# A two-block forward pass: four plain feature tiles ahead of the second feed-forward's seven-product stage, and three low halves of its activation sums made by GpSimd

## The chip, the core and the metric

The kernel runs on one core of a Trainium2 chip. The metric is the time of the device in microseconds (us), from the first to the last instruction of the program with the little that lies around it; lower is better. The engines of the core are named as in the profile: PE is the matrix engine (TensorE), PEld its weight loads, DVE is VectorE, ACT is ScalarE, POOL is GpSimd, SP (SyncE) issues most of the transfers.

## What is computed

The program is a forward pass of two blocks over 512 tokens of width 1024, all in float32. The first block has a modulated RMS norm, a convolution branch, a chunked mLSTM and a feed-forward. The second block has retention and latent attention, a feed-forward and a gated embedding. The change touches the feed-forward of the second block alone:

```
hn = rmsnorm(h, pre_ffn_norm[i])
ff = (jax.nn.silu(hn @ w_gate[i]) * (hn @ w_up[i])) @ w_down[i]
h = h + rmsnorm(ff, post_ffn_norm[i])
```

`hn` is 512 x 1024, `w_gate` and `w_up` are 1024 x 2816, so 22 feature tiles of 128 columns each.

## The kernel before

**Precision.** A float32 product is made of three passes. Each operand is split into a high half (`sph` for weights, `HH` for activations) and a low half, which is what is left of it (`spl`, `HL`), and PE adds high x high, low x high and high x low. ACT makes the high half of a weight tile by a copy, DVE the low half by a subtraction. A tile's row may hold several buffers of the same name (`raw`, `sph`, `spl`, `sums`): weights land in four `raw` buffers, their halves go into three `sph` and `spl` buffers.

**Plain feature tiles.** For feature tile f a unit of `w_gate` and a unit of `w_up` (128 x 1024 each) are multiplied with all 512 tokens: 24 matmuls of 512 columns for each, `hl` at lines 1884 and 1885 and `lo` at line 1892. DVE takes the gate out of its bank (`up_gate`, L2817), ACT applies silu and later rounds the product to `midh` (L2342), DVE multiplies (`up_`, L2828), and POOL makes the low half `midl` (L3169).

**Seven-product feature tiles.** For the other features, gate and up weights are seen as a 2 x 2 block (gate or up, first or second half of the 1024 inputs) and the activations as a 2 x 2 block (half of the inputs, half of the tokens). Their product is made of seven block products in place of eight, each of 12 matmuls of 256 columns (`seven`, L1922, L1924 and L1932), which is 84 matmuls for a feature. `SEVEN[2] = (5, 22)` says that features 5 to 21 of the second block go this way and 0 to 4 the plain way. `SEVEN_STEP` is the order in which the seven products of a feature are made. Each product needs

- its weight operand: the bare halves of a `raw` buffer or sums of them. A feature takes one accumulating transfer on POOL's queue (`seven_third`, L3130) and three sums on DVE (`seven_sum`, L2772, L2775, L2778), then a high half on ACT (`seven_high`, L2284) and a low half on DVE (`seven_low`, L2788) for each of the seven;
- its activation operand: bare quarters of `HH` and `HL`, or one of four sums of quarters. These four are made once for the stage: the sum `ts` on DVE (`seven_t_sum`, L2751 to L2759), its high half `th` on ACT (`seven_t_high`, L2272), its low half `tl` on DVE (`seven_t_low`, L2764), each 128 x 1024. `tl` lies where its `ts` lay, for number 0 to 2. `ts` 1 is worked out from `ts` 0, and `ts` 3 from `ts` 1. Products 1, 2, 4 and 6 of a feature (counted from 0 in the order made) use activation sums 0, 1, 2 and 3.

**What sets the order.** `plan()` writes one list of steps, and each engine runs its own steps of that list in this order; semaphores do the rest. `halves_2(n)` is called after plain tile n (even: gate, odd: up) has been taken out of its bank, and puts the steps for the activation sums between the plain tiles. The first five plain tiles (three gates and two ups) are multiplied before any is taken out, the normalising row of all tokens being late; the others follow one by one. A weight unit's `raw` buffer is loaded again once both halves of what was in it are made.

The plain tiles of this stage are multiplied from about 1140 us on, the seven-product features from 1191.15 us to 1362.68 us, and then `w_down` follows.

Of the kernel before, what the change touches and what calls it, by code (L numbers as in the profile page):

```python
# [7 lines left out]
ALU = mybir.AluOpType  # L8
ACT = mybir.ActivationFunctionType
AX = mybir.AxisListType  # L10
F32 = mybir.dt.float32
# [51 lines left out]

MIX_WORK = (2, 3)

SEVEN = {1: (3, 22), 2: (5, 22)}
SEVEN_STEP = (0, 3, 2, 4, 5, 1, 6)
SEVEN_SUMS = (2, 3, 4)

# [19 lines left out]
class Signals:  # L89
# [11 lines left out]
    def up(self, name, *labels, by=1):  # L101
        self.count[name] = self.count.get(name, 0) + by
        for label in labels:
            assert label not in self.now, label
            self.now[label] = (name, self.count[name])
        return self.sem(name), by

    def at(self, *label):
        if not self.known:
            return None  # L110
        name, value = self.known[label]
        return self.sem(name), value
# [18 lines left out]
def plan():  # L131
# [750 lines left out]
    def begin_seven(which):  # L882
        f0, f1 = SEVEN[which]
        st = {"which": which, "first": W["used"] + 2 * f0 + sum(st["slots"] - st["units"] for st in stages), "units": 2 * (f1 - f0),
# [77 lines left out]
    def ffn_up(which, acts, names, hook=None):  # L962
# [18 lines left out]
        for i in range(NFT):  # L981
            jobs += part(i)
        f0, f1 = SEVEN[which]

        def halves_2(n):
            if n in (2 * f0 - 4, 2 * f0 - 2):
                add("seven_third", which, (n - 2 * f0 + 4) // 2)
            if n == 0:
                add("seven_t_sum", which, 0)
                add("seven_t_high", which, 0)  # L990
            elif n == 2:
                ready()
                add("seven_t_sum", which, 1)
                add("seven_t_low", which, 0)
                add("seven_t_high", which, 1)
            elif n == 3:
                add("seven_t_sum", which, 3)
            elif n == 4:
                ready(more=1)
                add("seven_t_low", which, 1)  # L1000
            elif n == 5:
                add("seven_t_sum", which, 2)
                add("seven_t_high", which, 2)
            elif n == 6:
                add("seven_t_low", which, 2)

        def halves(n):
# [494 lines left out]
def program(nc, A, out, known):  # L1502
    steps, units = plan()
    ctx = ExitStack()
    with ctx:
        G = Signals(lambda name: ctx.enter_context(nc.semaphore(name)), known)
        up, at = G.up, G.at
# [44 lines left out]
        TH, TL, TS = [], [], []  # L1552
# [907 lines left out]
        def _(e):  # L2460
            w = Waited(e, G)
            up, fence = follow("DVE")
# [297 lines left out]
                ins.then_inc(*up("s_cut", ("seven_t_sum", which, t)))  # L2760

            def seven_t_low(which, t):
                w.wait_ge(at("seven_t_high", which, t))
                e.tensor_tensor(TL[t], TS[t][:], TH[t].bitcast(F32),  # L2764
                                ALU.subtract).then_inc(*up("s_cut", ("seven_t_low", which, t)))
# [329 lines left out]
        def _(e):  # L3095
            w = Waited(e, G)
            up, fence = follow("POOL")
# [23 lines left out]
            def x_reload(which, half):  # L3121
# [2 lines left out]
                e.dma_start(XT[:, 4 * half:4 * half + 4, :], A["x_scratch"][:, 4 * half:4 * half + 4, :]).then_inc(  # L3124
                    *G.up(f"d_xb{half}", ("x_back", which, half), by=16))

            def seven_third(which, i):
                n = seven_at[which][0] + 2 * i
                w.wait_ge(at("raw", n), at("raw", n + 1))
                e.dma_start(raw_half(n + 1, 0), raw_half(n, 0), accum_op=ALU.add).then_inc(  # L3130
                    *G.up(f"d_third{i % 2}", ("seven_third", which, i), by=16))
# [47 lines left out]
            def mix_ret():  # L3179
                for h in (1, 3):  # L3180
# [2 lines left out]
                        *up("s_cut_p", ("lo", "mix", h)))  # L3183

            run({"begin": begin, "zero_pads": zero_pads, "split": split, "sum": total, "v_begin": v_begin, "decay_begin": decay_begin, "m_out": m_out, "m_rows": m_rows,
                 "x_reload": x_reload, "seven_third": seven_third, "seven_mid_low": seven_mid_low,
                 "normlo": normlo, "up": up_, "rope_full": rope_full, "mix_ret": mix_ret,
                 "fence": fence})

# [129 lines left out]
```

## Time and profile before

| | us |
|---|---|
| median of three runs | 1541.39 |
| the three runs | 1541.39, 1543.04, 1539.12 |
| the profiled execution | 1539.65 |
| its span, first to last instruction | 1537.5 |
| PE busy | 1516.3 (99%) |
| DVE busy | 1136.2 (74%) |
| ACT busy | 799.4 (52%) |
| POOL busy | 150.3 (10%) |

The span is what the trace covers; the execution's own time has 2.15 us more. The shares are averages over a program of many stages, so that a stage is read from its own rows. A matmul's row has a length that reaches beyond the start of the next one, since matmuls are pipelined: what a matmul costs is read from the starts of two rows.

### The profile page before, as it was taken

What the parts mean: (1) busy time and instruction counts of PE and PEld (TensorE: products, weight loads), DVE (VectorE), ACT (ScalarE), POOL (GpSimd) and SP (SyncE); (2) the same over time, 40 slices, a digit from 0 to 9 for tenths busy, and PEclk for the clock granted to TensorE, in tenths of its full rate; (3) what the DMA queues carried; (4) which work ended last, traced back from release to release, by engine and by line L of the source; (5) the groups of instructions that cost most, each with busy time, mean ns of one, the idle gap of its engine ahead of it and who ended that gap; (6) DMA issues with size and microseconds to landing.
All of it is one profiled execution on the core that took longest, in us unless ns stands there. A gap on an engine that the chain in (4) does not pass through costs nothing.

```text
span 1537.5 us, 21554 instructions
## 1 busy us (share of the span) xinstructions
PE 1516.3 (99%) x8220; PEld 1290.2 (84%) x8220; DVE 1136.2 (74%) x1842; ACT 799.4 (52%) x1281; POOL 150.3 (10%) x158
## 2 busy tenths in 40 slices
PE   8999999999999999999999999999999999999998
PEld 3788777777788899999888887778888999998877
DVE  8999988898887789977673546766577888854356
ACT  5545477764553656666433335446455666643223
POOL 0111000000000101111021011010202111100100
PEclk9999999999999999999999999999999999999999
DMA  9788221223566546666623323111325565573331
GB/s 370 183 189 208 75 85 63 88 83 101 201 237 212 167 116 189 197 159 165 187 95 103 110 85 110 62 49 36 108 84 190 145 163 144 158 247 103 100 137 69
DMA packets 66344, 214.10 MB, mean 139 GB/s; under 512 B 7741, under 2 KB 10045, under 8 KB 65218
## 3 DMA queue, kind: packets, MB, share of 16 engines
q1 hardware_dynamic: 52496, 179.68, 34.2%
q0 software_dynamic: 13744, 33.04, 11.3%
q8 instruction: 65, 1.06, 0.3%
q14 instruction: 37, 0.30, 0.1%
q10 hardware_dynamic: 2, 0.00, 0.0%
HBM read 175.99 MB, written 8.40 MB: 120 GB/s over the span
## 4 chain that ended last, share of the span: by engine, by line
PE 84%; DVE 9%; ACT 4%; issue 2%; DMA 1%; ACTq 0%; DVEq 0%; SPq 0%
PE bank L1884 16%; PE bank L1892 16%; PE bank L1885 16%; PE bank L1922 8%; PE bank L1932 8%; PE bank L1924 8%; PE bank L1950 2%; DVE convout L2538 2%; PE bank L1962 1%; PE bank L1964 1%; PE bank L1963 1%; DVE spl L2476 1%; PE bank L2054 1%; PE bank L2067 1%; PE bank L2037 1%
## 5 line engine op out<-in xcount | busy, mean ns | idle before, releaser
L1884 PE MATMUL bank<-HH,sph 128*128 128x512 f32 x856 | 343.7, 402 | 5.6 <-DVE spl L2476 1.7
L1885 PE MATMUL bank<-HH,spl 128*128 128x512 f32 x856 | 333.9, 390 | 0.0
L2476 DVE TENSOR_TENSOR spl<-raw,sph 128x1024 fp32r<-128x1024 f32 (+1 forms) x165 | 205.1, 1245 | 165.5 <-ACT sph L2112 165.2
L2112 ACT ACTIVATE sph<-raw 128x1024 fp32r<-128x1024 f32 (+1 forms) x185 | 189.0, 1025 | 150.8 <-PE bank L1892 117.5
L1892 PE MATMUL bank<-HL,sph 128*128 128x512 f32 x856 | 226.1, 396 | 0.0
L1884 PEld LDWEIGHTS bank<-HH,sph 128*128 128x128 f32 x856 | 160.8, 188 | 45.9 <-issue 7.8
L1885 PEld LDWEIGHTS bank<-HH,spl 128*128 128x128 f32 x856 | 160.8, 188 | 34.7 <-issue 1.7
L1892 PEld LDWEIGHTS bank<-HL,sph 128*128 128x128 f32 x856 | 159.6, 188 | 34.6 <-issue 1.4
L2538 DVE SCALAR_TENSOR_TENSOR convout<-convin,vecs,convout 128x512 f32<-128x512 f32 x240 | 166.0, 742 | 0.0
L1922 PE MATMUL bank<-HH,sph 128*128 128x256 f32 x576 | 144.7, 283 | 0.1
L1924 PE MATMUL bank<-HH,spl 128*128 128x256 f32 x576 | 144.4, 283 | 0.0
L1884 PE MATMUL bank<-midh,sph 128*128 128x512 f32 x352 | 137.1, 389 | 0.0
L1885 PE MATMUL bank<-midh,spl 128*128 128x512 f32 x352 | 137.0, 389 | 0.0
L1922 PEld LDWEIGHTS bank<-HH,sph 128*128 128x128 f32 x576 | 110.5, 192 | 0.6 <-ACT tmp L2294 0.3
L1924 PEld LDWEIGHTS bank<-HH,spl 128*128 128x128 f32 x576 | 110.5, 192 | 0.1
L1922 PE MATMUL bank<-th,sph 128*128 128x256 f32 x432 | 108.4, 283 | 0.2 <-ACT tmp L2289 0.2
L1924 PE MATMUL bank<-th,spl 128*128 128x256 f32 x432 | 108.3, 283 | 0.0
L2788 DVE TENSOR_TENSOR spl<-raw,sph 128x512 fp32r<-128x512 f32 x144 | 97.1, 694 | 11.8 <-ACT sph L2284 11.7
L2284 ACT ACTIVATE sph<-sums 128x512 fp32r<-128x512 f32 x108 | 63.4, 622 | 69.7 <-DVE sums L2775 69.7
L1932 PE MATMUL bank<-HL,sph 128*128 128x256 f32 x576 | 92.6, 283 | 0.0
L2284 ACT ACTIVATE sph<-raw 128x512 fp32r<-128x512 f32 x144 | 89.7, 624 | 4.6 <-PE bank L1932 1.2
L1892 PE MATMUL bank<-midl,sph 128*128 128x512 f32 x352 | 87.6, 389 | 0.0
(365 smaller groups left out, 2688.3 us busy)
## 6 DMA issues: line engine op xcount, KB each, us to landing
raw<-in_w_in SPq DMA_DIRECT2D x69, 512.0 KB, 3.2
raw<-in_w_up SPq DMA_DIRECT2D x66, 512.0 KB, 4.4
more<-in_w_ada SPq DMA_DIRECT2D x32, 512.0 KB, 5.7
raw<-in_w_down SPq DMA_DIRECT2D x32, 512.0 KB, 3.7
raw<-in_w_gate SPq DMA_DIRECT2D x22, 512.0 KB, 3.5
raw<-raw POOLq DMA_DIRECT2D x36, 256.0 KB, 4.4
midl<-tmp POOLq DMA_DIRECT2D x36, 256.0 KB, 3.3
spl<-raw POOLq DMA_DIRECT2D x17, 512.0 KB, 5.5
```

Of the source, the lines that this page charges most:

```text
L1884: e.matmul(P_[b][:], sph(n)[:, q], hi[:, k, :], start=k == 0, stop=False)
L1885: e.matmul(P_[b][:], spl(n)[:, q], hi[:, k, :], start=False, stop=False)
L1892: m = e.matmul(P_[b][:], sph(n)[:, q], low[:, k, :], start=False, stop=last and k == kb - 1)
L1922: e.matmul(to, high_of(which, s)[:, q], x, start=begins and k == 0, stop=False, skip_group_check=not begins)
L1924: e.matmul(to, low_of(which, s)[:, q], x, start=False, stop=False, skip_group_check=not begins)
L1932: m = e.matmul(to, high_of(which, s)[:, q], x, start=False, stop=k == 3, skip_group_check=not begins)
L1950: m = e.matmul(P_[b][:], raw(n)[:, token(k)], FULL[acts][:, k, :], start=k == 0, stop=k == 7)
L2112: e.activation(sph(n), raw(n), ACT.Copy).then_inc(*up("s_w_high", ("wh", n)))
L2284: e.activation(high_of(which, s), given, ACT.Copy).then_inc(*up("s_w_high", ("seven_high", which, s), *labels))
L2476: e.tensor_tensor(spl(n), raw(n), sph(n).bitcast(F32), ALU.subtract).then_inc(*up("s_w_low", ("wl", n)))
L2538: ins = e.scalar_tensor_tensor(CO[:, i, :], src, wt, CO[:, i, :], ALU.mult, ALU.add)
L2788: e.tensor_tensor(low_of(which, s), given, high_of(which, s).bitcast(F32), ALU.subtract).then_inc(*up("s_w_low", ("seven_low", which, s), ...
```

## The change

`SEVEN[2]` becomes `(4, 22)`: feature 4 is made by seven products and no longer by two plain tiles, so the stage has four plain features and eighteen of the other kind. `halves_2` puts the low half of activation sum 2 with its sum and high half, at n = 5, where it stood at n = 6. The low halves of activation sums 0, 1 and 2 move from DVE to POOL, with waits on the sums that read the same memory before it is overwritten. In the first feed-forward nothing changes.

```diff
-SEVEN = {1: (3, 22), 2: (5, 22)}
+SEVEN = {1: (3, 22), 2: (4, 22)}
+POOL_LOWS = (0, 1, 2)
...
             elif n == 5:
                 add("seven_t_sum", which, 2)
                 add("seven_t_high", which, 2)
-            elif n == 6:
                 add("seven_t_low", which, 2)
...
             def seven_t_low(which, t):
+                if which == 2 and t in POOL_LOWS:
+                    return
                 w.wait_ge(at("seven_t_high", which, t))
...
+            def seven_t_low(which, t):
+                if which == 2 and t in POOL_LOWS:
+                    w.wait_ge(at("seven_t_high", which, t))
+                    if t < 2:
+                        w.wait_ge(at("seven_t_sum", which, (1, 3)[t]))
+                    e.tensor_tensor(TL[t], TS[t][:], TH[t].bitcast(F32),
+                                    ALU.subtract).then_inc(*up("s_cut_p", ("seven_t_low", which, t)))
```

The last function stands among POOL's steps.

On DVE, from activation sum 1 (`ts_101`) on, before; `tmp` rows take plain tiles out of their banks, `spl` rows of 128x1024 belong to plain units:

```order
L2754 SCALAR_TENSOR_TENSOR ts_101<-pf,ts_98 128x1024
L2764 TENSOR_TENSOR tl_97<-ts_98,th_96 128x1024
L2828 TENSOR_TENSOR tmp_91<-tmp_91,bank 128x512
L2759 SCALAR_TENSOR_TENSOR ts_105<-pf,ts_101 128x1024
L2817 TENSOR_TENSOR tmp_90<-bank,rrow 128x512
L2476 TENSOR_TENSOR spl_63<-raw_56,sph_60 128x1024
L2764 TENSOR_TENSOR tl_100<-ts_101,th_99 128x1024
L2828 TENSOR_TENSOR tmp_90<-tmp_90,bank 128x512
L2756 TENSOR_TENSOR ts_104<-pf 128x1024
L2476 TENSOR_TENSOR spl_61<-raw_57,sph_58 128x1024
L2817 TENSOR_TENSOR tmp_87<-bank,rrow 128x512
L2764 TENSOR_TENSOR tl_103<-ts_104,th_102 128x1024
```

and after:

```order
L2754 SCALAR_TENSOR_TENSOR ts_101<-pf,ts_98 128x1024
L2830 TENSOR_TENSOR tmp_91<-tmp_91,bank 128x512
L2759 SCALAR_TENSOR_TENSOR ts_105<-pf,ts_101 128x1024
L2819 TENSOR_TENSOR tmp_90<-bank,rrow 128x512
L2476 TENSOR_TENSOR spl_63<-raw_56,sph_60 128x1024
L2830 TENSOR_TENSOR tmp_90<-tmp_90,bank 128x512
L2756 TENSOR_TENSOR ts_104<-pf 128x1024
L2790 TENSOR_TENSOR spl_61<-raw_57,sph_58 128x512
L2819 TENSOR_TENSOR tmp_87<-bank,rrow 128x512
L2774 TENSOR_TENSOR sums_65<-raw_54 128x512
L2777 TENSOR_TENSOR sums_64<-sums_65,raw_57 128x512
L2780 TENSOR_TENSOR sums_65<-raw_57,sums_65 128x512
```

The three `tl` rows are gone, and behind activation sum 2 (`ts_104`) the operands of the first seven-product feature follow at once.

On POOL, from the low half of plain feature 0 (`midl<-tmp_89`) on, before; the DMA rows are the accumulating transfers of `seven_third`:

```order
L3169 TENSOR_TENSOR midl<-tmp_89,midh 128x512
L3169 TENSOR_TENSOR midl<-tmp_91,midh 128x512
L3169 TENSOR_TENSOR midl<-tmp_90,midh 128x512
L3130 DMA raw_56<-raw_55 128x512
L3169 TENSOR_TENSOR midl<-tmp_87,midh 128x512
L3130 DMA raw_54<-raw_57 128x512
L3169 TENSOR_TENSOR midl<-tmp_86,midh 128x512
```

and after:

```order
L3179 TENSOR_TENSOR midl<-tmp_89,midh 128x512
L3134 TENSOR_TENSOR tl_97<-ts_98,th_96 128x1024
L3179 TENSOR_TENSOR midl<-tmp_91,midh 128x512
L3140 DMA raw_54<-raw_57 128x512
L3134 TENSOR_TENSOR tl_100<-ts_101,th_99 128x1024
L3179 TENSOR_TENSOR midl<-tmp_90,midh 128x512
L3134 TENSOR_TENSOR tl_103<-ts_104,th_102 128x1024
L3140 DMA raw_56<-raw_55 128x512
L3179 TENSOR_TENSOR midl<-tmp_87,midh 128x512
```

The low halves of the activation sums now stand between those of the plain features, and the first accumulating transfer stands two places earlier.

On ACT, from the high half of activation sum 2 (`th_102`) on, before:

```order
L2272 ACTIVATE th_102<-ts_104 128x1024
L2112 ACTIVATE sph_58<-raw_57 128x1024
L2335 ACTIVATE tmp_87<-tmp_87 128x512
L2112 ACTIVATE sph_59<-raw_54 128x1024
L2342 ACTIVATE midh<-tmp_87 128x512
L2284 ACTIVATE sph_60<-raw_55 128x512
L2335 ACTIVATE tmp_86<-tmp_86 128x512
```

and after:

```order
L2272 ACTIVATE th_102<-ts_104 128x1024
L2284 ACTIVATE sph_58<-raw_57 128x512
L2335 ACTIVATE tmp_87<-tmp_87 128x512
L2284 ACTIVATE sph_58<-sums_64 128x512
L2284 ACTIVATE sph_59<-sums_65 128x512 x2
L2284 ACTIVATE sph_60<-raw_54 128x512
L2342 ACTIVATE midh<-tmp_87 128x512
```

The high half of the first seven-product operand (`sph_58<-raw_57`, 128x512) is now the next instruction behind `th_102`.

## Rows read from the trace of the kernel before

**Rows 1.** The page: the span, and the granted PE clock in 40 slices

```profile
span 1537.5 us, 21554 instructions
...
PEclk9999999999999999999999999999999999999999
```

**Rows 2.** Timeline of PE: start us, length us, line, operation, count, [idle before <-releaser]

```profile
1174.01 0.47 PE L1884 MATMUL bank<-HH,sph 128*128 128x512 f32 x1
...
1177.73 1.98 PE L1892 MATMUL bank<-HL,sph 128*128 128x512 f32 x8
1180.18 0.47 PE L1884 MATMUL bank<-HH,sph 128*128 128x512 f32 x1 [0.47 <-DVE spl L2476]
...
1183.89 1.98 PE L1892 MATMUL bank<-HL,sph 128*128 128x512 f32 x8
1185.71 0.39 PE L1884 MATMUL bank<-HH,sph 128*128 128x512 f32 x1
...
1191.15 0.28 PE L1922 MATMUL bank<-HH,sph 128*128 128x256 f32 x1
...
1192.58 0.28 PE L1922 MATMUL bank<-th,sph 128*128 128x256 f32 x1
...
1362.68 0.40 PE L1884 MATMUL bank<-midh,sph 128*128 128x512 f32 x1
```

**Rows 3.** Timeline of DVE in the plain tiles and the first seven-product operands

```profile
1165.21 1.21 DVE L2754 SCALAR_TENSOR_TENSOR ts<-pf,ts 128x1024 f32<-128x1024 f32 x1
1166.34 2.32 DVE L2764 TENSOR_TENSOR tl<-ts,th 128x1024 fp32r<-128x1024 f32 x1
1168.58 0.67 DVE L2828 TENSOR_TENSOR tmp<-tmp,bank 128x512 f32<-128x512 f32 x1
...
1172.64 1.23 DVE L2476 TENSOR_TENSOR spl<-raw,sph 128x1024 fp32r<-128x1024 f32 x1 [1.65 <-ACT sph L2112]
1173.78 1.22 DVE L2764 TENSOR_TENSOR tl<-ts,th 128x1024 fp32r<-128x1024 f32 x1
...
1185.32 1.38 DVE L2788 TENSOR_TENSOR spl<-raw,sph 128x512 fp32r<-128x512 f32 x1 [1.22 <-ACT sph L2284]
...
1187.22 0.68 DVE L2772 TENSOR_TENSOR sums<-raw 128x512 f32<-128x512 f32 x1
...
1189.39 1.89 DVE L2788 TENSOR_TENSOR spl<-sums,sph 128x512 fp32r<-128x512 f32 x3
...
1197.10 0.69 DVE L2772 TENSOR_TENSOR sums<-raw 128x512 f32<-128x512 f32 x1
```

**Rows 4.** Timeline of POOL in the same stretch, and its one subtraction of 128x1024, at the end

```profile
1165.70 1.88 POOL L3169 TENSOR_TENSOR midl<-tmp,midh 128x512 fp32r<-128x512 f32 x1 [45.17 <-ACT midh L2342]
...
1177.83 0.87 POOL L3130 DMA_DIRECT2D raw<-raw  x1
1184.86 1.28 POOL L3169 TENSOR_TENSOR midl<-tmp,midh 128x512 fp32r<-128x512 f32 x1 [6.16 <-ACT midh L2342]
```

```profile
1484.69 2.35 POOL L3110 TENSOR_TENSOR spl<-raw,sph 128x1024 fp32r<-128x1024 f32 x1 [14.61 <-ACT sph L2112]
```

**Rows 5.** Timeline of POOL and of DVE earlier, where both had low halves queued

```profile
1080.61 3.00 POOL L3182 TENSOR_TENSOR HL<-rg,HH 128x512 fp32r<-128x512 f32 x2 [50.59 <-ACT HH L2414]
```

```profile
1081.09 1.37 DVE L3018 TENSOR_TENSOR HL<-rg,HH 128x512 fp32r<-128x512 f32 x1 [0.35 <-ACT HH L2414]
```

**Rows 6.** Timeline of ACT: a silu, and high halves

```profile
1171.03 0.63 ACT L2335 ACTIVATE tmp<-tmp 128x512 f32<-128x512 f32 x1 [1.10 <-DVE tmp L2817]
1171.56 1.04 ACT L2112 ACTIVATE sph<-raw 128x1024 fp32r<-128x1024 f32 x1
...
1176.77 1.06 ACT L2272 ACTIVATE th<-ts 128x1024 fp32r<-128x1024 f32 x1 [0.50 <-DVE ts L2756]
```

**Rows 7.** Lines 3130 and the weight loads: from issue to landing, us

```profile
DMA to landing us min/median/max: 3.2/4.4/5.7
```

```profile
DMA to landing us min/median/max: 3.2/3.7/7.8
```

More of the change, by code:

```diff
@@ L3185, in _ @@
             run({"begin": begin, "zero_pads": zero_pads, "split": split, "sum": total, "v_begin": v_begin, "decay_begin": decay_begin, "m_out": m_out, "m_rows": m_rows,
-                 "x_reload": x_reload, "seven_third": seven_third, "seven_mid_low": seven_mid_low,
+                 "x_reload": x_reload, "seven_t_low": seven_t_low, "seven_third": seven_third, "seven_mid_low": seven_mid_low,
                  "normlo": normlo, "up": up_, "rope_full": rope_full, "mix_ret": mix_ret,
```

## The prediction, made before the changed kernel was run

> **What bounds the kernel now.** I read the page first: the span is 1537.5 us, and the clock that PE was granted is full in every slice [rows 1]. Then the timeline of PE over the end of the plain tiles and the start of the seven products. From 1191.15 to 1362.68 us, 17 features take 171.53 us, 10.09 us each, and product 1 starts 1.43 us after product 0 [rows 2]; the page puts PE at 99% busy. So PE bounds this stage, and DVE, ACT and POOL count only where PE would have to wait for one of their results. Third, the timelines of DVE, POOL and ACT from 1165 us on, read against PE's: by when is each half made, and by when is it wanted.
>
> **The gain on PE.** The last two plain tiles, feature 4, start at 1180.18 us and the seven products at 1191.15: 10.97 us. Ahead of them PE lost more. A group of eight L1892 takes 1.82 us from its start to the next matmul (1183.89 to 1185.71), so the tile could have started at 1177.73 + 1.82 = 1179.55 us; it started 0.63 us later, behind a wait for `spl` [rows 2]. Feature 4 thus costs 11.60 us now. By seven products it costs 10.09. If no half is late, the change gives 1.51 us. Nothing else on PE changes.
>
> **How POOL and DVE get along.** Three rows decide what the move to POOL costs. DVE's `tl` at 1166.34 takes 2.32 us where its twin at 1173.78 takes 1.22. POOL was in a subtraction until 1165.70 + 1.88 = 1167.58, and the slow `tl` ended 1.08 us after that. Likewise the `spl` at 1185.32 takes 1.38 us: POOL's subtraction from 1184.86 ended at 1186.14, 0.56 us before it [rows 3, 4]. And POOL's own 1.88 us (1.28 alone) are 1.16 us from the end of DVE's `ts` at 1166.42. So a DVE operation with both inputs in SBUF and a subtraction on POOL exclude each other, from first to last element. Operations with one input in a bank, such as L2828, I take as free of it. Who comes next when both queue, shows at 1080.61: two POOL subtractions take 3.00 us, not 2.58, and a DVE low half waits from 1081.09 to 1082.46; it ran between the two [rows 5]. They take turns. The Trainium skill says of this ("SBUF — State Buffer", the section on the two separate sides of SBUF) that DVE and GpSimd share a port pair as an exclusive lock, taken against GpSimd by DVE operations with two SBUF inputs, and that the loser blocks fully. By that rule, the trace agrees; a reader who took POOL as an engine that runs beside DVE would keep the gain of 1.51 us, which is rival 1.
>
> A subtraction of 128x1024 takes 2.35 us on POOL [rows 4] and 1.22 on DVE [rows 3], of which 1.14 lie between two in a row. Three of them are 7.05 us of POOL time, in which DVE's two-input operations stand still, for 3.66 us of DVE's own work. The Trainium skill ("GPSIMD Engine Reference", the section on instruction dispatch) gives about 2.5 cycles for an element of a two-input operation at 1.2 GHz, which makes 2.13 us of 1024; the row has 2.35, and goes. With 2.13 the waits below would be some 0.4 us shorter.
>
> **The walk.** Up to `ts` 1 (ends 1166.42) all orders are as before. From there I put each instruction at the latest of its inputs, its engine's queue and the lock, in the order shown in the part on the change.
> - Lock: POOL `midl` of feature 0 until 1167.58; DVE `ts` 3, waiting since 1166.94, until 1168.66; POOL `tl` 0, 2.23 us behind it, until 1170.89; POOL `midl` 1 (ready since 1168) until 1172.1, just ahead of DVE's `spl` of the last plain tile, whose high half ACT ends at 1170.9. That `spl` ends at 1173.2 (1173.87 before), in time for PE's tile at 1174.01 [rows 2, 3].
> - POOL issues the accumulating transfer for feature 4 at 1172.1 (0.87 us) and takes the lock for `tl` 1 from 1173.2 to 1175.4. DVE, done with L2828 at 1173.8, has `ts` 2 queued behind this: 1175.4 to 1176.5; before, `th` 2 followed it at 1176.77 [rows 6]. It has hardly become earlier, though the stage that wants it has, by 11 us.
> - ACT's queue is in order: `th` 2 (1.06 us [rows 6]) until 1177.65, and only then the high half of product 0's weights, until 1178.2. At 1177.7 `th` 2 also releases `tl` 2 on POOL, whose queue is empty by then (`midl` 2 ran 1176.5 to 1177.66). So POOL holds the lock from 1177.7 to 1180.05, and the low half of product 0, ready for DVE at 1178.2, ends at 1180.05 + 0.56 = 1180.6. PE begins 0.14 us behind a low half (1173.87 and 1174.01 [rows 2, 3]). **First wait:** product 0 starts at 1180.75 instead of 1179.55, 1.2 us.
> - Behind this low half stand L2817 (0.60 us) and the three weight sums. The first starts at 1181.15. Before, the low half of product 1 was ready 2.85 us after the first sum began: 1187.22, 1189.39 and a third of the three [rows 3]. That makes 1184.0. **Second wait:** product 1 could follow at 1180.75 + 1.43 = 1182.2 and starts at 1184.1, 1.9 us.
> - The next low halves come 0.6 us apart against 1.43 on PE, so products 2 and 3 do not wait. `midl` 3 on POOL (about 1186.6 to 1187.8) delays the low half of product 5 to 1188.4; it is wanted at 1189.9. The high and low half of activation sum 3 are wanted at 1191.3 and ready by 1190.2.
> - Feature 5: DVE starts its sums at about 1190.8, so the low half of its product 1 is ready at about 1194.0 and wanted at 1192.8 + 1.43 = 1194.2. Just in time; before, DVE was 2.5 us ahead here. From then on the features are those of before.
>
> **The sum.** 10.09 + 1.2 + 1.9 = 13.2 us for feature 4 against 11.60: **1.6 us slower**. The profiled span would be 1539.1 and its execution 1541.2 us. That execution (1539.65) lies 1.7 us below the median of the three runs, so on the median I put 1541.39 + 1.6 = **1543.0 us**. About 0.3%, 4.6 us, is what a measurement of this kernel can tell from no change: the outcome I expect is no measurable difference.
>
> **Nothing or little elsewhere.** The three low halves that DVE loses cost PE nothing before; DVE had idle time in front of `spl` at 1172.64 [rows 3], and what it is spared is refilled by the lock. The accumulating transfer of feature 4 lands 3.2 to 5.7 us after its issue [rows 7], at 1175.3 to 1177.8 from 1172.1, and the first sum that reads it comes at 1181.15. The weights of feature 6 are loaded once the low halves of products 5 and 6 are made, 1188.4 and 1189.0; with 4.4 us of landing each time (medians 3.7 and 4.4 [rows 7]) the transfer that adds them has landed at 1198, and DVE wants it at 1192.75 + 5.95 = 1198.7 (1197.10 against 1191.15 before [rows 2, 3]). It is hidden, with under 1 us to spare. At the end of the stage PE went over to `w_down` without a wait at 1362.68, and an even number of products (126 for 119) frees the weight slots no later.
>
> **Rivals.**
> 1. *The lock costs less than I hold.* If `ts` 2 gets ahead of `tl` 1, or the low halves on POOL keep DVE out only in part, `th` 2 ends up to 1.6 us earlier and so does all behind it; with no exclusion at all the low half of product 1 is ready at 1179.7, before it is wanted (1181.0). Then the gain of 1.51 us stands: 1539.9 us. For it: the walk has near ties (1170.89 against 1170.9 for `midl` 1 and `spl`), and one tie that falls the other way moves a wait by about 1.2 us. Against it: both directions of the exclusion are in rows 3 to 5. With one wait gone and the other left the result is within 0.5 us of before.
> 2. *The feed of the weights becomes the bound: slower by more than 0.3%.* DVE's lead over PE, 2.5 us before, is used up at feature 5. If loads take 7.8 us and the adding transfer 5.7, the ends of rows 7, feature 6's sums start 1189.0 + 7.8 + 5.7 + 0.2 = 1202.7 instead of 1198.7, the low half comes at 1205.5, and PE wants it at 1192.75 + 10.09 + 1.43 = 1204.3: 1.2 us more for that feature. It decides once the two landings together exceed 12.3 us, and it comes to over 4.6 us only if it strikes three features: 1.6 + 3.6 = 5.2 us, 1546.6. Against it: both medians together are 8.1 us, and 7.8 is the largest of the stretch.
> 3. *Adding transfer late for feature 4 itself*, beyond 1181.15: it would need 9 us to land, which no row has. I fold it into rival 2.
>
> **Chances.** Forecast, two waits of 2.4 to 4 us together (+0.9 to +2.5 us): 0.55. Rival 1, with its half-way cases (-1.5 to +0.9): 0.32. Rival 2 in any strength: 0.10, a third of it short of 4.6 us. What is in none of them, such as buffers of other numbers behind the stage: 0.03. Range: from rival 1's end less the spread of a median (the runs lie 2.3 us below and 1.7 above) to rival 2's single stall, 1.6 + 1.2 = 2.8, plus the same: 1541.39 - 1.5 - 1.4 = 1538.5 to 1541.39 + 2.8 + 1.8 = 1546.0. Faster by over 0.3% needs 4.6 us where the whole gain is 1.51: 0.03. Slower by over 0.3%: rival 2's strong case: 0.07. Within: 0.90.
>
> **What would show it.** In the profile after, PE's first L1922 at 1180.7 with a wait of about 1.1 us for the low half (L2790), and a second of nearly 2 us ahead of the first matmul on `th`. POOL's `tl` rows of 2.2 to 2.9 us, with DVE's `ts` 3, `ts` 2, `spl` and the low half of product 0 lengthened next to them by the time that POOL is in one. `ts` 2 ending at about 1176.5. No waits of PE in the later features. Wrong it would be if DVE's rows keep their 1.2 and 0.7 us beside POOL's (rival 1), or if DVE waits for `raw` in features 6 to 8 and PE with it (rival 2).

## The result, and the profile after

| | before | after |
|---|---|---|
| median, us (19 runs each) | 1539.81 | 1543.95 |
| span of the profiled execution, us | 1537.5 | 1541.1 |
| PE, DVE, ACT, POOL busy, us | 1516.3, 1136.2, 799.4, 150.3 | 1516.1, 1141.4, 802.8, 159.6 |

The ratio is 1.0024, with a 95% interval of 1.0017 to 1.0030: the changed kernel is slower by 2.6 to 4.6 us, 3.7 in the middle. That is within the 0.3% that the prediction called no measurable difference, but the interval leaves out 1: with 19 runs of each, the loss is told from no change. I had put it at 1.6 us. One execution of the kernel before took 1964.02 us where the other 18 lie between 1538.95 and 1543.04; it hardly moves the median, and the ratio is of the undisturbed runs.

The timeline of PE of the changed kernel has three waits where the plain tiles hand over to the seven products (columns as in [rows 2]):

```profile
1177.54 1.98 PE L1892 MATMUL bank<-HL,sph 128*128 128x512 f32 x8
1180.80 0.36 PE L1922 MATMUL bank<-HH,sph 128*128 128x256 f32 x1 [1.28 <-DVE spl L2790]
...
1184.14 0.36 PE L1922 MATMUL bank<-th,sph 128*128 128x256 f32 x1 [1.67 <-issue]
...
1187.35 0.39 PE L1922 MATMUL bank<-th,sph 128*128 128x256 f32 x1 [1.55 <-ACT tmp L2289]
...
1189.09 0.39 PE L1922 MATMUL bank<-HH,sph 128*128 128x256 f32 x1
...
1194.94 0.28 PE L1922 MATMUL bank<-HH,sph 128*128 128x256 f32 x1
```

These are products 0, 1, 2 and 3 of feature 4, and the first of feature 5. The last plain tile ends at 1177.54 + 1.82 = 1179.36 us, the point from which I count from here on. A product takes 1.44 us. So product 0 is 1.44 late, product 1 starts 3.34 after it (1.90 lost), product 2 3.21 (1.77 lost), product 3 1.74 (0.30 lost), product 4 another 0.09. Feature 4 took 1194.94 - 1179.36 = 15.58 us, against 11.60 before: 4.0 us more, and the spans differ by 3.6 (0.2 of the rest is that the plain tiles ended that much earlier, 1179.36 for 1179.55). Behind it no feature has a wait, so the whole loss lies in these 16 us.

DVE in the same stretch, from activation sum 3 to the low halves of feature 4 (compare [rows 3]):

```profile
1166.88 1.73 DVE L2759 SCALAR_TENSOR_TENSOR ts<-pf,ts 128x1024 f32<-128x1024 f32 x1
...
1170.86 2.35 DVE L2476 TENSOR_TENSOR spl<-raw,sph 128x1024 fp32r<-128x1024 f32 x1 [1.65 <-ACT sph L2112]
1173.13 0.68 DVE L2830 TENSOR_TENSOR tmp<-tmp,bank 128x512 f32<-128x512 f32 x1
1173.73 2.82 DVE L2756 TENSOR_TENSOR ts<-pf 128x1024 f32<-128x1024 f32 x1
1178.20 2.46 DVE L2790 TENSOR_TENSOR spl<-raw,sph 128x512 fp32r<-128x512 f32 x1 [1.65 <-ACT sph L2284]
...
1181.18 0.68 DVE L2774 TENSOR_TENSOR sums<-raw 128x512 f32<-128x512 f32 x1
...
1183.35 1.90 DVE L2790 TENSOR_TENSOR spl<-sums,sph 128x512 fp32r<-128x512 f32 x3
1185.16 0.68 DVE L2830 TENSOR_TENSOR tmp<-tmp,bank 128x512 f32<-128x512 f32 x1
```

POOL (compare [rows 4]):

```profile
1167.49 3.39 POOL L3134 TENSOR_TENSOR tl<-ts,th 128x1024 fp32r<-128x1024 f32 x1
...
1172.67 2.80 POOL L3134 TENSOR_TENSOR tl<-ts,th 128x1024 fp32r<-128x1024 f32 x1
1175.43 2.28 POOL L3179 TENSOR_TENSOR midl<-tmp,midh 128x512 fp32r<-128x512 f32 x1
1177.72 2.38 POOL L3134 TENSOR_TENSOR tl<-ts,th 128x1024 fp32r<-128x1024 f32 x1
```

A low half of 128x512 that takes 0.68 us alone took 2.46 at 1178.20: POOL was in its third `tl` until 1180.10, and the low half ended 0.56 us later. `ts` 2 took 2.82 us where it took 1.22 before, since POOL's second `tl` was in its way. The 3.39 and 2.28 us of POOL are the other direction: POOL waited for DVE.

The third wait is ACT's. Its timeline (compare [rows 6]):

```profile
1184.26 0.61 ACT L2284 ACTIVATE sph<-raw 128x512 fp32r<-128x512 f32 x1
1185.88 0.63 ACT L2342 ACTIVATE midh<-tmp 128x512 fp32r<-128x512 f32 x1 [1.00 <-DVE tmp L2830]
1186.41 0.61 ACT L2284 ACTIVATE sph<-raw 128x512 fp32r<-128x512 f32 x1
1186.93 0.36 ACT L2289 ACTIVATE tmp<-bank 128x256 f32<-128x256 f32 x1
...
1187.72 1.05 ACT L2272 ACTIVATE HH<-ts 128x1024 fp32r<-128x1024 f32 x1
1188.67 0.37 ACT L2294 ACTIVATE tmp<-bank 128x256 f32<-128x256 f32 x1
```

L2289 is `seven_first`: ACT copies product 0 out of its bank, and product 2 is made in the same bank (the code lets it begin only behind this copy). Product 0 was finished by 1182.24 us, its copy began at 1186.93, and PE followed the copy's end (1187.29) at 1187.35. The copy stood in ACT's queue behind `midh` of plain feature 3, which waited for DVE's L2830 at 1185.16, which stood in DVE's queue behind the three low halves of 1183.35. In the same way product 3 (1189.09) followed the copy L2294 of product 1, which stood behind `HH<-ts`.

### The profile page after: what moved, and what is told of

Same layout as the page of the kernel before. It is cut to its first block, busy times and chain, and to the rows that moved or that the text cites. A ratio compares the mean times of both kernels' runs of the same rounds, so it can differ in the third digit from the quotient of the medians.

```text
span 1541.1 us, 21653 instructions
## 1 busy us (share of the span) xinstructions
PE 1516.1 (98%) x8256; PEld 1291.6 (84%) x8256; DVE 1141.4 (74%) x1850; ACT 802.8 (52%) x1290; POOL 159.6 (10%) x162
## 3 DMA queue, kind: packets, MB, share of 16 engines
q8 instruction: 66, 1.08, 0.3%
## 4 chain that ended last, share of the span: by engine, by line
PE 83%; DVE 9%; ACT 4%; issue 2%; DMA 1%; ACTq 0%; DVEq 0%; SPq 0%
PE bank L1884 16%; PE bank L1892 15%; PE bank L1885 15%; PE bank L1922 8%; PE bank L1932 8%; PE bank L1924 8%; PE bank L1950 2%; DVE convout L2538 2%; PE bank L1962 1%; PE bank L1964 1%; PE bank L1963 1%; DVE spl L2476 1%; PE bank L2054 1%; PE bank L2067 1%; PE bank L2037 1%
## 5 line engine op out<-in xcount | busy, mean ns | idle before, releaser
L1884 PE MATMUL bank<-HH,sph 128*128 128x512 f32 x840 | 337.2, 401 | 5.1 <-DVE spl L2476 1.3
L1885 PE MATMUL bank<-HH,spl 128*128 128x512 f32 x840 | 327.6, 390 | 0.0
L1892 PE MATMUL bank<-HL,sph 128*128 128x512 f32 x840 | 222.1, 396 | 0.0
L1922 PE MATMUL bank<-HH,sph 128*128 128x256 f32 x592 | 148.8, 284 | 1.4 <-DVE spl L2790 1.3
L1924 PE MATMUL bank<-HH,spl 128*128 128x256 f32 x592 | 148.4, 283 | 0.0
L1922 PE MATMUL bank<-th,sph 128*128 128x256 f32 x444 | 111.6, 284 | 3.4 <-ACT tmp L2289 1.8
L2790 DVE TENSOR_TENSOR spl<-raw,sph 128x512 fp32r<-128x512 f32 x148 | 100.9, 702 | 12.2 <-ACT sph L2284 12.2
L1922 PEld LDWEIGHTS bank<-th,sph 128*128 128x128 f32 x444 | 85.2, 192 | 4.0 <-ACT tmp L2289 2.2
```

What stands on the lines that cost most here:

```text
L1884: e.matmul(P_[b][:], sph(n)[:, q], hi[:, k, :], start=k == 0, stop=False)
L1885: e.matmul(P_[b][:], spl(n)[:, q], hi[:, k, :], start=False, stop=False)
L1892: m = e.matmul(P_[b][:], sph(n)[:, q], low[:, k, :], start=False, stop=last and k == kb - 1)
L1922: e.matmul(to, high_of(which, s)[:, q], x, start=begins and k == 0, stop=False, skip_group_check=not begins)
L1924: e.matmul(to, low_of(which, s)[:, q], x, start=False, stop=False, skip_group_check=not begins)
L2790: e.tensor_tensor(low_of(which, s), given, high_of(which, s).bitcast(F32), ALU.subtract).then_inc(*up("s_w_low", ("seven_low", which, s), ...
```

## The experiments

Each run is compared with runs of the kernel before on the same chip, so a ratio is always to the kernel before. Since the ratios are known to 0.1% only (1.4 us), I read the mechanism from PE's timeline: the starts of products 0 to 3, counted from the end of the last plain tile, and the time until the next feature starts. On time they would be 0, 1.4, 2.9, 4.3 and 10.1. The span of one profiled execution also holds what happened elsewhere, so that it need not follow the column before it; e1_lows_dve is the plainest case.

| run | products 0, 1, 2, 3 | next feature | against before, us | span, us | ratio, 95% interval |
|---|---|---|---|---|---|
| before (feature 4 plain) | | 11.60 | | 1537.5 | |
| after | 1.44, 4.78, 7.99, 9.73 | 15.58 | +4.0 | 1541.1 | 1.0024 [1.0017, 1.0030] |
| e1_lows_dve | 0.25, 3.59, 6.80, 8.54 | 14.40 | +2.8 | 1541.1 | 1.0019 [1.0009, 1.0028] |
| e2_five_plain | | 12.96 | +1.4 | 1539.1 | 1.0007 [0.9998, 1.0016] |
| e3_late_high | 1.43, 4.76, 6.34, 8.92 | 14.77 | +3.2 | 1540.0 | 1.0015 [1.0006, 1.0025] |
| e5_no_read | 0.0, 1.43, 3.49, 5.23 | 11.09 | -0.5 | 1537.2 | 0.9990 [0.9980, 0.9999] |
| e6_in_gaps | 0.0, 1.43, 3.32, 4.85 | 11.57 | 0.0 | 1537.3 | 0.9998 [0.9989, 1.0007] |
| e7_early_up | 1.44, 4.78, 7.30, 8.84 | 15.03 | +3.4 | 1540.2 | 1.0017 [1.0008, 1.0027] |
| e8_last_on_dve | 0.0, 3.01, 7.35, 9.53 | 16.13 | +4.5 | 1542.5 | 1.0026 [1.0016, 1.0035] |
| e9_copy_first | 0.0, 1.42, 4.21, 5.72 | 11.48 | -0.1 | 1537.1 | 0.9994 [0.9985, 1.0004] |
| e10_copy_between | 0.0, 1.42, 2.86, 4.33 | 10.62 | -1.0 | 1536.6 | 0.9988 [0.9979, 0.9997] |

**e1_lows_dve: the feature moved, the low halves left on DVE.**

```diff
-POOL_LOWS = (0, 1, 2)
+POOL_LOWS = ()
```

> Four plain feature tiles, but all low halves of the activation sums stay on DVE (POOL_LOWS empty). Theory A (DVE and POOL exclude each other, and each of three waits has its own cause): the wait before product 0 nearly goes (1.28 us to under 0.3), since the low half of product 0 comes at about 1179.6 us; the waits before products 1 and 2 stay at 1.5 to 1.9 us each, being due to the late weight sums and to ACT's queue. Span 2.4 to 3.0 us over before (the changed kernel: 3.6). Theory B (the move to POOL is harmless, the stage is only entered too early): span as in the changed kernel, 3.6 us over before, with a first wait of 1.3 us.

Measured: +2.8 us. The first wait is gone but for 0.25 us, since DVE makes `tl` 2 itself at 1177.89 and the low half of product 0 right behind it, at 1179.03. The other two waits are there in full. First DVE, then PE:

```profile
1177.89 1.23 DVE L2766 TENSOR_TENSOR tl<-ts,th 128x1024 fp32r<-128x1024 f32 x1 [1.13 <-ACT th L2272]
1179.03 0.69 DVE L2790 TENSOR_TENSOR spl<-raw,sph 128x512 fp32r<-128x512 f32 x1
```

```profile
1183.20 0.36 PE L1922 MATMUL bank<-th,sph 128*128 128x256 f32 x1 [1.67 <-issue]
...
1186.41 0.39 PE L1922 MATMUL bank<-th,sph 128*128 128x256 f32 x1 [1.55 <-ACT tmp L2289]
```

So of the 4.0 us the move to POOL carries 1.2, and the larger part comes from beginning the seven products with the low halves in this place at all, whichever engine makes them.

The span of this execution, 1541.1 us, is that of the changed kernel, which read alone would have spoken for Theory B. The gain in feature 4 was lost again later. PE began `w_down` 0.93 us ahead of the changed kernel (at 1365.37 against 1366.30), and was still about 0.8 ahead at the four L1988 of 128x512 (1488.78 against 1489.59). Just there the granted clock fell: it was 0.50 from 1489 to 1491 us, where the changed kernel had 1.00, and at 1492.5 both kernels were level.

**e2_five_plain: the low halves on POOL, the feature left plain.**

```diff
-SEVEN = {1: (3, 22), 2: (4, 22)}
+SEVEN = {1: (3, 22), 2: (5, 22)}
```

> Five plain feature tiles as before, but the low halves of activation sums 0 to 2 on POOL. Theory A: the wait of PE before the last gate tile grows from 0.5 us (0.63 by the starts) to about 1.6, since POOL's subtraction for sum 2 keeps DVE from the low half of that tile until about 1180.1; no wait in the seven products. Span 1.0 to 1.2 us over before. Theory B: span as before, within 0.3 us.

Measured: +1.4 us, where 1.0 to 1.2 was expected. The products have no wait; the last gate tile has one, for a low half that POOL's third `tl` (1178.17, 2.38 us) lengthens from 1.23 to 2.56 us. First PE, then DVE:

```profile
1181.78 0.47 PE L1884 MATMUL bank<-HH,sph 128*128 128x512 f32 x1 [1.79 <-DVE spl L2476]
```

```profile
1179.07 2.56 DVE L2476 TENSOR_TENSOR spl<-raw,sph 128x1024 fp32r<-128x1024 f32 x1 [2.08 <-ACT sph L2112]
```

The two parts apart cost 2.8 and 1.4 us, which is 4.2; both together cost 4.0, so they add up nearly.

**e5_no_read: POOL writes `tl` and reads nothing.** The low parts of activation sums 0, 1 and 2 are left out.

```diff
-                    e.tensor_tensor(TL[t], TS[t][:], TH[t].bitcast(F32),
-                                    ALU.subtract).then_inc(*up("s_cut_p", ("seven_t_low", which, t)))
+                    e.memset(TL[t].bitcast(F32), 0.0).then_inc(*up("s_cut_p", ("seven_t_low", which, t)))
```

> The changed kernel, but POOL fills the three low halves with zeros in place of subtracting, so it reads nothing there; the low parts of activation sums 0 to 2 are left out of the result. Theory A (the lock is the root of the late operands, also of the third wait): none of the three waits of PE is left, span 1.4 to 1.6 us under before. Theory B (the first operands are late by the order alone): the second and third wait stay, span 2 to 3.6 us over before. If POOL's filling with zeros excludes DVE as well, DVE's rows beside it are longer by up to its own length of about 1 us, and something between the two comes out.

Measured: the first two waits are gone, and DVE's rows beside POOL's fills are no longer than alone (`ts` 3 still took 1.73 us, for `midl` of feature 0, which reads). The low half of the last plain unit ran from 1171.43 to 1172.66 with POOL's fill going on until 1172.11; DVE first, then POOL:

```profile
1171.43 1.23 DVE L2476 TENSOR_TENSOR spl<-raw,sph 128x1024 fp32r<-128x1024 f32 x1 [1.65 <-ACT sph L2112]
```

```profile
1168.03 0.96 POOL L3134 MEMSET tl<- 128x1024 f32 x1
...
1170.86 1.25 POOL L3134 MEMSET tl<- 128x1024 f32 x1
```

The same low half took 2.35 us in the changed kernel, beside a subtraction. So the exclusion does not go with every operation of POOL: this one, which only writes, leaves DVE alone. (The fill is shorter than the subtraction as well, so the 4.5 us between this run and the changed kernel are not the price of the exclusion alone.) One thing was missed: I expected no wait to be left and a gain of 1.4 to 1.6 us, and it was 0.5 us. ACT's copy of product 0 still held product 2 for 0.6 us, and the next copy product 3 for 0.3. This showed the third wait to be a cause of its own, that hides behind the second and outlives it.

**e3_late_high: `midh` of feature 3 behind the first copy in ACT's queue.** The diff leaves out the new step itself, which is the `midh` instruction of `up_`, unchanged.

```diff
                 add("seven_first", which, i, sum_bank(i)[0], gate[i], free)
+                if which == 2 and i == 0:
+                    add("late_high", f0 - 1, late[0])
...
             def up_(which, i, b, g, j):
+                if which == 2 and i == SEVEN[2][0] - 1:
+                    return
                 w.wait_ge(at("up_done", which, i))
```

> The changed kernel, with one instruction moved in ACT's queue: the rounding of the last plain feature (midh, L2342) stands behind the copy of product 0 out of its bank (L2289) and not ahead of it. Theory A (product 2 waits for this copy, which queues behind a rounding that waits for DVE): the copy ends at about 1185.7 us and not 1187.3, the third wait falls from 1.55 us to about 0.1, span 1.9 to 2.2 us over before. Theory B (product 2 waits for its own operands): span as in the changed kernel, 3.6 us over before.

Measured: the copy began at 1185.05 and product 2 started 1.58 us behind product 1 (3.21 in the changed kernel), so the cause of the third wait is named rightly. But the gain was 0.8 us and not 1.6 or more. `midh`, a high half and `HH<-ts`, 2.3 us together, now stood between the two copies, and the second held product 3:

```profile
1188.04 0.39 PE L1927 MATMUL bank<-HH,sph 128*128 128x256 f32 x1 [0.89 <-ACT tmp L2299]
```

**e7_early_up: DVE takes the up tile of feature 3 out behind the first low half, so that `midh` is ready sooner; activation sum 3 is split two steps later.**

```diff
             def first_sums(b, g):
+                if which == 2:
+                    factors(st, 4)
+                    freed = evac(b, g)
+                    factors(st, 5)
+                    return freed
                 factors(st, 5)
...
-            if s == 1:
+            if s == (3 if which == 2 else 1):
                 add("seven_t_high", which, 3, plain)
-            elif s == 2:
+            elif s == (4 if which == 2 else 2):
                 add("seven_t_low", which, 3)
```

> The changed kernel with the low halves left on POOL; only the last plain product is taken out behind the low half of product 1 and not of product 3, and activation sum 3 is rounded two steps later. Theory A: the waits ahead of products 0 and 1 stay (starts 1.4 and 4.8 us behind the last plain tile), those ahead of products 2 and 3 go; feature 4 takes 13.4 to 13.6 us (the changed kernel: 15.58; the prediction had 13.2), 1.8 to 2.0 us over before. Theory B (product 2 waits for its own low half): product 2 starts 7.5 us or more behind the last plain tile, feature 4 takes 15 us or more.

Measured: 15.03 us, 1.5 more than expected. `midh` came 1.2 us earlier (1184.31; counted from the end of the last plain tile, as all of this), but two high halves stand between it and the copy, which therefore began only 0.7 us earlier. Product 2 was still 1.08 us late, and product 6 another 0.33.

**e8_last_on_dve: `tl` 2 back on DVE, behind the low halves of products 1 to 3.**

```diff
-POOL_LOWS = (0, 1, 2)
+POOL_LOWS = (0, 1)
...
-                add("seven_t_low", which, 2)
...
                 factors(st, 5)
+                if which == 2:
+                    add("seven_t_low", which, 2)
                 return evac(b, g)
```

> The changed kernel, but the low half of activation sum 2 is made by DVE, behind the low halves of products 1 to 3; POOL keeps sums 0 and 1. Theory A (POOL's last subtraction alone keeps product 0 waiting): product 0 starts within 0.1 us of the end of the last plain tile, product 1 about 1.6 us late and product 2 again 1.5 us late, feature 4 takes 13.3 to 14.0 us, 1.7 to 2.4 us over before. Theory B (the delay comes from the earlier two): product 0 still starts 1 us or more late.

Measured: product 0 on time and product 1 1.58 us late, both as expected. From product 2 on the forecast failed: the feature took 16.13 us where 13.3 to 14.0 was expected. I had again not followed the queue. `tl` 2 (1184.30, 1.22 us) stands ahead of the up tile's L2831, that ahead of `midh`, and that ahead of the copy:

```profile
1187.62 0.39 PE L1923 MATMUL bank<-th,sph 128*128 128x256 f32 x1 [2.68 <-ACT tmp L2290]
```

Product 2 lost 2.90 us against 1.77 in the changed kernel. The 1.13 more are what `tl` 2 put ahead of the chain, although the low half of product 2 was ready by 1184: this chain, and no low half, sets product 2.

Products 3 and 4 were late by another 0.74 and 0.85 us, and most of that is no wait. The granted clock was 0.50 from 1188.6 to 1191.6 us, the lower of its two levels, behind a stretch (1184.0 to 1187.6) in which PE had been busy for 0.95 of 3.6 us. The matmuls of product 3 are 0.21 us apart there, those of product 4 again 0.12:

```profile
1189.80 0.42 PE L1923 MATMUL bank<-HH,sph 128*128 128x256 f32 x1
...
1192.09 0.28 PE L1923 MATMUL bank<-th,sph 128*128 128x256 f32 x1
```

In the changed kernel, at full clock, the same two products were late by 0.30 and 0.09 us, so about 1.2 us of the 16.13 are the clock's (an estimate from these two). Without it the feature would have taken some 14.9 us, less than the 15.58 of the changed kernel: taking `tl` 2 from POOL gave back more at products 0 and 1 (1.44 and 0.32 us) than it cost at product 2.

**e6_in_gaps: four plain features, every low half on DVE, put where DVE is idle or ahead of its queue.** With the edits of e7_early_up, and besides:

```diff
-POOL_LOWS = (0, 1, 2)
+POOL_LOWS = ()
...
-                add("seven_t_low", which, 0)
...
             elif n == 4:
+                add("seven_t_low", which, 0)
                 ready(more=1)
-                add("seven_t_low", which, 1)
             elif n == 5:
                 add("seven_t_sum", which, 2)
                 add("seven_t_high", which, 2)
-                add("seven_t_low", which, 2)
+                add("seven_t_low", which, 1)
...
                     factors(st, 5)
+                    add("seven_t_low", which, 2)
                     return freed
```

> Four plain feature tiles; all low halves of the activation sums on DVE, number 0 in its gap ahead of the last plain weight tile, number 1 behind sum 2, number 2 behind the low halves of products 1 to 3; the last plain product is taken out of its bank behind the low half of product 1 and not of product 3; activation sum 3 is rounded two steps later. Theory A (three waits: lock, late weight sums, ACT's copy behind a rounding): none of the three is left, feature 4 takes 10.1 to 10.4 us from the end of the last plain tile (before: 11.60, the changed kernel: 15.58), so 1.2 to 1.5 us less than before, 5.2 to 5.5 less than the changed kernel. Theory B (the stage is entered before DVE can have its operands, whatever their order): a wait of 1 us or more ahead of product 1 stays, and the time is that of before or more.

Measured: the first two waits are gone, and feature 4 costs what it costs in the kernel before, 11.57 us; 10.1 to 10.4 was expected. Two waits were left. The copy of product 0, behind `midh` and two high halves, held product 2 by 0.46 us; and my own edit had put the low half of activation sum 3 (1187.99, 1.22 us) ahead of DVE's reading of product 4's bank (L2800, 1189.13), which product 6 needs:

```profile
1182.87 0.38 PE L1927 MATMUL bank<-th,sph 128*128 128x256 f32 x1 [0.29 <-ACT tmp L2294]
...
1189.60 0.38 PE L1927 MATMUL bank<-HH,sph 128*128 128x256 f32 x1 [0.71 <-DVE tmp L2800]
```

**e9_copy_first: e6_in_gaps, with both of these changed.** Against it:

```diff
                     freed = evac(b, g)
-                    factors(st, 5)
                     add("seven_t_low", which, 2)
...
                 add("seven_up", which, i, sum_bank(i)[0], up[i])
+                if which == 2 and i == 0:
+                    add("seven_t_low", which, 3)
...
-            factors(st, s + 6)
+            if which == 1 or s:
+                factors(st, s + 6)
...
-            elif s == (4 if which == 2 else 2):
+            elif s == 2 and which == 1:
                 add("seven_t_low", which, 3)
```

> The kernel of the run e6_in_gaps (four plain feature tiles, all low halves of the activation sums in VectorE's gaps) with its two leftover waits taken away: ScalarE's copy of product 0 stands ahead of the high halves of products 4 and 5 instead of behind them, and the low half of activation sum 3 stands behind the reading of product 4's bank (the up tile's sum) instead of ahead of it. If the chain copy of product 0 behind ScalarE's queue is what was missing in the forecast, product 2 starts on time (2.9 us after the last plain tile, before 3.32), product 6 starts 8.7 (before 10.05), and feature 4 takes 10.1 to 10.3 us against 11.6 in the kernel before: 1.2 to 1.5 us under it, ratio 0.9990 to 0.9992. If instead the seven products cannot be fed by the two vector engines at this point at all (a wait is always passed on to the next product), a new wait of 0.5 us or more appears within the first seven products and the feature stays at 10.7 or more.

Measured: 11.48 us. Product 6 was no longer held up, but product 2 started at 4.21 instead of 2.9. With the call to `factors` I had also moved the low halves of products 2 and 3 behind `tl` 2; the first of them began at 1181.86, took 1.78 us beside POOL's `midl` (1181.57 to 1183.10) and ended at 1183.64, and product 2 started at 1183.74, 0.10 us behind it; the copy of product 0 had been done since 1181.74. Read alone, this run would have spoken for the rival that a wait is always passed on.

**e10_copy_between: e6_in_gaps, with the low halves of products 2 and 3 left in place.** Against e6_in_gaps:

```diff
                 add("seven_up", which, i, sum_bank(i)[0], up[i])
+                if which == 2 and i == 0:
+                    add("seven_t_low", which, 3)
...
-            factors(st, s + 6)
+            factors(st, s + (5 if which == 2 and s < 3 else 6))
...
-            elif s == (4 if which == 2 else 2):
+            elif s == 2 and which == 1:
                 add("seven_t_low", which, 3)
```

> As e9_copy_first, but the low halves of products 2 and 3 stand ahead of the low half of sum 2 on VectorE again (in e9_copy_first my edit had put them behind it, and product 2 then waited for its low half until 1183.7). The kernel is e6_in_gaps with the copy of product 0 behind one high half (product 4's) instead of two, the high halves of products 5 and 6 each one place later, and the low half of sum 3 behind the reading of product 4's bank. Expected by the theory that the copies' place in ScalarE's queue and that one low half are all that was missing: products at 0.0, 1.4, 2.9, 4.3, 5.8, 7.2, 8.6, the next feature at 10.1 to 10.3 against 11.6 before, ratio near 0.999. By the rival (a wait is always passed on): one wait of 0.4 us or more remains, next feature at 10.6 or later.

Measured: 10.62 us, 1.0 under the kernel before, median 1538.80 us against 1540.77. The interval of the ratio, 0.9979 to 0.9997, leaves out 1: this version beats the kernel before by a little (0.5 to 3.2 us) and the changed one by more. Products 1 to 5 are on time within 0.05 us, because ACT's copies now come as soon as their products are done:

```profile
1181.12 0.63 ACT L2349 ACTIVATE midh<-tmp 128x512 fp32r<-128x512 f32 x1 [0.32 <-DVE tmp L2837]
1181.66 0.61 ACT L2291 ACTIVATE sph<-raw 128x512 fp32r<-128x512 f32 x1
1182.18 0.36 ACT L2296 ACTIVATE tmp<-bank 128x256 f32<-128x256 f32 x1
1182.45 0.62 ACT L2291 ACTIVATE sph<-raw 128x512 fp32r<-128x512 f32 x1
1182.97 0.38 ACT L2301 ACTIVATE tmp<-bank 128x256 f32<-128x256 f32 x1
```

What is left is 0.5 us about product 6: it waits 0.3 us for DVE's L2802, which stands behind two sums of feature 5, and the rest follows in the same product, whose last four matmuls begin as `HL<-ts` ends. By the letter of the expectation the rival's bound (10.6 or later) is met, though none of the waits reaches its 0.4 us. Of the 5.5 us that PE lost in feature 4 of the changed kernel (15.58 against 10.08), 5.0 are gone, so waits are not always passed on in their size.

## Why the prediction was right or wrong

**What bounds the stage: right.** Feature 4 with nothing late would take 10.1 us, e10_copy_between reached 10.6, and in no run did PE wait in the features behind.

**How POOL and DVE get along: right, in both directions.** POOL's three rows in question grew to 3.39, 2.80 and 2.28 us and DVE's to 2.35, 2.82 and 2.46, at the places that the walk gave. e5_no_read is the test by experiment: beside a fill of POOL, which only writes, DVE's `spl` kept its 1.23 us. The Trainium skill ("SBUF — State Buffer", the section on the two separate sides) limits the lock to a GpSimd operation that reads SBUF; the trace agrees.

**The first wait: right.** `tl` 0 to end at 1170.89, the last plain `spl` at 1173.2, `ts` 2 at 1176.5, the low half of product 0 at 1180.6 and product 0 at 1180.75: the trace has 1170.88, 1173.21, 1176.55, 1180.66 and 1180.80. The near tie that rival 1 lived on (1170.89 against 1170.9) fell as I had put it. One term was read where it could not be seen: the matmul at 1174.01 had no wait, and would have begun at 1172.18 + 1.82 = 1174.00 anyway, so the 0.14 us behind a low half did not follow from it. The row at 1180.18 has the same 0.14 behind a low half that ended at 1180.04, and so has product 0 after. e1_lows_dve gives the price of the lock for this wait: 1.2 us.

**The second wait: right,** 1184.1 forecast, 1184.14 measured, though not the lock alone makes it. e1_lows_dve has it in full without POOL. It is DVE's order, low half of product 0, up to the sums, the high half and the next low half, that takes 2.85 us from the first sum and begins too late. With `tl` 2 behind these low halves instead of ahead of them (e8_last_on_dve) product 1 was still 1.58 us late. What comes too late there is `ts` 2, which stands behind `tl` 1 on DVE or waits for it on POOL; its high half `th` 2 in turn stands ahead of product 0's high half on ACT. e6_in_gaps, with `tl` 1 behind `ts` 2 and `tl` 2 behind the low halves, has no such wait: against e1_lows_dve it changed nothing but the order.

**"Products 2 and 3 do not wait": wrong, and the step that failed.** I had walked what product 2 reads, its low half, and had left out where it is written. Its bank is free once ACT has copied product 0. The same chain is in the trace of before, one feature later, and I had not followed it there. ACT:

```profile
1192.07 0.64 ACT L2342 ACTIVATE midh<-tmp 128x512 fp32r<-128x512 f32 x1
1192.61 0.61 ACT L2284 ACTIVATE sph<-raw 128x512 fp32r<-128x512 f32 x1
1193.13 0.36 ACT L2289 ACTIVATE tmp<-bank 128x256 f32<-128x256 f32 x1
```

The copy ended at 1193.49 and PE began product 2 at 1194.02: half a microsecond to spare, and in my own walk the second wait already showed DVE that much behind. In the first feed-forward of the kernel before, whose stage begins the same way, PE even waits for this copy:

```profile
552.92 0.38 PE L1922 MATMUL bank<-th,sph 128*128 128x256 f32 x1 [0.21 <-ACT tmp L2289]
```

Price in the changed kernel: 1.77 us for product 2, 0.30 for product 3, 0.09 for product 4, 2.2 together. My 13.2 us plus 2.2 make 15.4; the trace has 15.58, the rest being the 0.24 us by which product 0 started later counted from the plain tiles' end (1.44 for 1.2), since these ended at 1179.36 and not at 1179.55.

**Landings and rival 2: right.** Nothing waited for `raw` in features 5 and 6. The margin I gave feature 5 ("just in time") was not tested, since the third wait moved PE back by 2 us. In e5_no_read and e10_copy_between, where PE was early, no wait appeared there either.

**The total.** The direction held and the size did not: +1.6 forecast, +3.7 (2.6 to 4.6) by the ratio, +4.0 by the place itself. The bound of 0.3% covered the miss. That the time itself, 1543.0 us forecast and 1543.95 measured, came within 1 us is luck: I had added 1.6 us to a median of three runs, 1541.39, and the median of 19 is 1539.81, so a start 1.6 us too high made up for most of the wait that I left out. Rival 1, to which I had given 0.32, had a false premise, the weak exclusion. Its consequence fails too: e5_no_read, which comes nearest to it, has the first two waits gone, but gained 0.5 us and not 1.5, for the copy that I had left out of both walks.

## What to carry to other kernels

When a walk checks that an operand arrives in time, it must walk what frees the place it is written to as well: here PE's third wait was for a 0.36 us copy out of a bank, behind a `midh` behind a DVE instruction that had nothing to do with it. A wait hides the next one behind it, so a stage shortened by one cause shows its gain only when the others are gone too (e6_in_gaps 0.0 us, e10_copy_between 1.0 us, on the same idea). And where DVE has gaps in the right places, they are cheaper than a second engine that locks DVE out: the low halves cost at most 0.5 us there (e10_copy_between), and 1.2 to 1.4 us on POOL (e1_lows_dve against the changed kernel, e2_five_plain).

## What the runs showed of the hardware

- A fill of 128x1024 on POOL (MEMSET, e5_no_read) runs beside a DVE subtraction with two inputs in SBUF: DVE's took 1.23 us, as long as without it. The subtraction of the same size takes 2.38 us on POOL and shuts DVE out until its end. I had not weighed in the prediction that reading and writing could differ.
- Of the three fills one, at 1170.86, took 1.25 us and the others, at 1168.03 and 1175.54, 0.96. All three had a two-input operation of DVE beside them for a part of their time, so that alone does not account for it. The slow one follows POOL's issuing of a transfer (1170.28, 0.87 us) directly; whether that is the reason was not tested.
- PE's granted clock fell from 1.00 to 0.50 for some 3.6 us in e8_last_on_dve, behind 3.6 us with PE busy for 0.95, and for some 3 us in e1_lows_dve, between 1488 and 1492, behind PE's short matmuls of one column (L2004 and L2007, 1485.57 to 1487.3). In the changed kernel it stayed at 1.00 through 1180.0 to 1187.3, with PE busy for 3.33 of 7.3 us. So a late start of a matmul isn't always a wait: the clock of the stretch has to be read first.
